# Dense single-pass products with unread results between the small products of TensorE

## The reference, cut to what matters

```
def step(S, inp):                       # one position, per head; S is 64 x 64
    r_t, w_t, k_t, v_t, a_t, b_t = inp
    sa = einsum('bhij,bhj->bhi', S, a_t)
    S = S * w_t + sa * b_t + v_t * k_t
    return S, einsum('bhij,bhj->bhi', S, r_t)
...
mu, var = mean(y), mean((y - mu)**2)    # over the 64 values of a head
y = (y - mu) * rsqrt(var + GN_EPS) * lnx_w + lnx_b
out = (y + bonus) * g                   # g = sigmoid(gd) @ gate_g2
```

## Time and profile before

| | us |
|---|---|
| median of 3 runs (lowest, highest) | 1946.46 (1945.67, 1948.81) |
| the profiled execution | 1947.46 |
| its span, first to last instruction | 1945.7 |
| TensorE busy | 1786.3 (92%) |
| VectorE busy | 973.9 (50%) |
| ScalarE busy | 484.3 (25%) |
| GpSimd busy | 271.0 (14%) |
| mean granted clock | 0.943 |

### The profile page before, as it was taken

One profiled execution on the slowest core, in us unless ns is written; L12 is line 12 of the kernel. 1 busy time (PEld: TensorE's weight loads), 2 busy tenths in 40 slices (PEclk: granted clock), 3 DMA queues, 4 the chain that ended last, 5 costly groups with the idle time before them and its releaser, 6 DMA issues. The chain is left out here.

```text
span 1945.7 us, 39461 instructions
## 1 busy us (share of the span) xinstructions
PE 1786.3 (92%) x17306; PEld 1601.8 (82%) x17306; DVE 973.9 (50%) x1730; ACT 484.3 (25%) x937; POOL 271.0 (14%) x357
## 2 busy tenths in 40 slices
PE   5999998997999758889979999999999999999996
PEld 4999994665666427888729999999999999999996
DVE  6233316775766385444344266445455455455455
ACT  6122113553222342222134321111111111111113
POOL 1000004324766030001011200000000000000000
PEclk8999998997999869999579999999999999999999
DMA  8211103102766200000042111110110111110203
GB/s 241 55 44 44 42 27 93 50 17 62 239 201 203 66 1 3 4 4 20 1 148 65 34 33 38 49 55 28 50 55 28 56 48 33 55 41 22 62 25 111
DMA packets 136613, 119.29 MB, mean 61 GB/s; under 512 B 16771, under 2 KB 123640, under 8 KB 136171
## 3 DMA queue, kind: packets, MB, share of 16 engines
q1 hardware_dynamic: 124507, 78.06, 13.6%
q0 software_dynamic: 11792, 38.17, 6.1%
q10 hardware_dynamic: 144, 0.52, 0.1%
HBM read 102.94 MB, written 11.44 MB: 59 GB/s over the span
## 5 line engine op out<-in xcount | busy, mean ns | idle before, releaser
L205 PE MATMUL bank<-normed2T_hi,w_hi 128*128 128x384 f32 (+1 forms) x1032 | 337.3, 327 | 0.0
L206 PE MATMUL bank<-normed2T_hi,w_lo 128*128 128x384 f32 (+1 forms) x1032 | 336.9, 326 | 0.0
L207 PE MATMUL bank<-normed2T_lo,w_hi 128*128 128x384 f32 (+1 forms) x1032 | 336.9, 326 | 0.0
L205 PEld LDWEIGHTS bank<-normed2T_hi,w_hi 128*128 128x128 f32 x1032 | 193.8, 188 | 1.6 <-issue 1.6
L207 PEld LDWEIGHTS bank<-normed2T_lo,w_hi 128*128 128x128 f32 x1032 | 193.8, 188 | 0.0
L206 PEld LDWEIGHTS bank<-normed2T_hi,w_lo 128*128 128x128 f32 x1032 | 193.8, 188 | 0.0
L205 PE MATMUL bank<-inner_hi,w_hi 128*128 128x384 f32 (+1 forms) x528 | 175.0, 331 | 10.2 <-DVE w_lo L494 7.1
L494 DVE TENSOR_TENSOR w_lo<-work,w_hi 128x1024 fp32r<-128x1024 f32 (+2 forms) x120 | 118.6, 989 | 130.6 <-ACT w_hi L489 129.4
L207 PE MATMUL bank<-inner_lo,w_hi 128*128 128x384 f32 (+1 forms) x528 | 174.7, 331 | 0.0
L206 PE MATMUL bank<-inner_hi,w_lo 128*128 128x384 f32 (+1 forms) x528 | 174.5, 330 | 0.0
L205 PE MATMUL bank<-normedT_hi,w_hi 128*128 128x384 f32 (+3 forms) x480 | 157.8, 329 | 5.6 <-DVE w_lo L494 5.6
(11 more groups left out here) (410 smaller groups left out, 3199.4 us busy)
## 6 DMA issues: line engine op xcount, KB each, us to landing
work<-in_w_up_dram SPq DMA_DIRECT2D x44, 512.0 KB, 3.9
work<-in_w_in_dram SPq DMA_DIRECT2D x19, 512.0 KB, 3.8
work<-in_w_down_dram SPq DMA_DIRECT2D x32, 256.0 KB, 2.7
residualT<-residual_spill SPq DMA_DIRECT2D x1, 4352.0 KB, 16.4
work<-in_x_prompt_dram SPq DMA_DIRECT2D x8, 512.0 KB, 5.6
residual_spill<-rwkv_streamsT SPq DMA_DIRECT2D x8, 512.0 KB, 4.4
work<-in_w_out_dram SPq DMA_DIRECT2D x8, 512.0 KB, 4.8
out_dram<-work SPq DMA_DIRECT2D x8, 512.0 KB, 2.7
```

What stands on the lines that cost most here:

```text
L205: pe.matmul(out, w[0], x[0], start=first, stop=False)
L206: pe.matmul(out, w[1], x[0], start=False, stop=False)
L207: return pe.matmul(out, w[0], x[1], start=False, stop=last)
```

## The change

A helper `keep_busy` issues `n` products of a dense 128 x 128 tile with 512 columns of the same tile in fp32r (single pass). Their results go to a PSUM bank that is free at that time and are overwritten before anybody reads it. The tile is filled once, by a copy on ScalarE at the start of the sample block; TensorE waits for it after the solve. In the sample part two such products go ahead of each product q of kinds 1 to 3 (18 places, 36 products), behind the wait for the bank and ahead of the other waits. In the mixing twelve go behind the first three gate products, ahead of the wait for the reciprocal, and one behind each of the nine spreading products. Nothing is removed or moved.

```
--- before.py
+++ after.py
@@ -205,6 +205,11 @@
             pe.matmul(out, w[0], x[0], start=first, stop=False)
             pe.matmul(out, w[1], x[0], start=False, stop=False)
             return pe.matmul(out, w[0], x[1], start=False, stop=last)
+
+        def keep_busy(pe, dense, bank, n):
+
+            for _ in range(n):
+                pe.matmul(bank[:, 0:512], dense[:, 0:P], dense[:, 0:512], start=True, stop=True, skip_group_check=True)
 
         def C(name):
             return con[:, CONST[name][0]:CONST[name][0] + CONST[name][1]]
@@ -2098,6 +2103,8 @@
             sem("sample_taken_act"), sem("sample_taken_dve"), sem("sample_values_spread"),
             sem("sample_states_added"), sem("sample_states_new"))
 
+        dense = lay("dense", RW + 768, 512, F32R)
+        s_dense = sem("dense_set")
         of_sequence = C("seq_of")[0:NS, :].unsqueeze(2).broadcast_to([NS, NB, HD])
 
         def s_taken(eng, q):
@@ -2131,6 +2138,7 @@
             @block.tensor
             def _(pe):
                 products(pe, sample_ops)
+                pe.wait_ge(s_dense, 1)
                 taken(pe, op(i8, "RT"))
                 for f in range(2):
                     taken(pe, op(i8, "AP", f))
@@ -2149,6 +2157,8 @@
                         rows, m = head(h)
                         x = zs.wu[:, h]
                         cols = slice(h * HD, (h + 1) * HD)
+                    if 1 <= what <= 3:
+                        keep_busy(pe, dense, b, 2)
                     if what == 0:
                         last = pe.matmul(b[rows, 0:NS], x[:, 0:HD], ident[:, 0:NS], start=True, stop=True)
                     elif what == 1:
@@ -2222,6 +2232,7 @@
 
             @block.scalar
             def _(act):
+                nc.scalar.copy(dense[:, :], con[:, 0:512]).then_inc(s_dense, 1)
                 take_act(act, sample_ops)
                 for q in range(18):
                     what, h = divmod(q, 6)
@@ -2307,6 +2318,7 @@
                 pe.wait_ge(g_sig, 2)
                 for j in range(3):
                     gate_product(j)
+                keep_busy(pe, dense, PS[0], 12)
                 pe.wait_ge(y_ri, 1)
                 for j, (m, c) in enumerate(jobs):
                     if j >= 2:
@@ -2314,6 +2326,7 @@
                     rows = slice(32 * c, 32 * c + 32)
                     pe.matmul(PS[3 + j % 2][:, 0:384], heads_in[rows, m, 32:], devs[rows], start=True, stop=True
                               ).then_inc(y_bc, 1)
+                    keep_busy(pe, dense, PS[0], 1)
                     if 3 <= j:
                         gate_product(j)
```

## The result

The changed kernel takes 1968.7 us (median of 4, 1964.18 to 1976.36) against 1946.31 (median of 4, 1945.67 to 1948.81): ratio 1.0117, 95% interval 1.008 to 1.0153, so 22.4 us slower. Forecast were 1950.0 with 1935 to 1967: the direction was right, the size was not, and the time lies 1.7 us outside the range. The right direction counts for little: the forecast was 3.5 us above the median of before, less than the 3.9 that the prediction itself calls just tellable from no change. The execution that was profiled took 1976.36 us (span 1974.5), 28.9 more than the profiled one of before, and was the slowest of the four; sizes read from it are those of a slow draw.

A forecast was written before the change was run, and what follows sets the result against it. It took TensorE, busy without gaps at half clock in the sample part, as the bound. Sample part +8.0 and mixing -5.5 made +2.5 on the profiled 1947.46 us, hence 1950.0, range 1935 to 1967.

The forecast's parts named there:

- The sample part: Products 6 to 17 at +6.7 us and products 18 to 23 with what follows at +1.3: +8.0 us.
- That the products of the sample part are path time: Sample part: TensorE is busy without waiting, so added products cannot hide in a wait and lengthen the path.
- I take it that the clock falls all the same, two groups later than now: Products 6 to 17: half clock returns despite the pairs; two more groups run at full clock, saving 1.9 us.
- The price of a pair: Two dense 512-column products cost 0.85 us at half clock or 0.45 at full, estimated by columns from 384-column products.
- I let the clock come back half way: Products 18 to 23: three turns at 0.85 + 0.1 us, three at 0.45 + 0.1, together 4.5, that is +3.1.
- the start of products 24 and 25 at full clock (-1.8): Sample part, up to the first new state: half of 3.68 us saved because the clock is back by then.
- Mixing, -5.5: Mixing: full clock in the second loop saves 6.7 us, less 1.2 for dense products overrunning their wait.
- The overrun: Mixing: twelve dense products take 2.7 us in a wait of 1.51, overrunning it by 1.2.
- The loop: Mixing's second loop: full clock after the twelve dense products, 9.2 us instead of 15.84, saving 6.7.
- Rival B: The mixing starts at half clock and stays there, +15.3 us on the forecast: 1965.3 us; chance 0.26.
- Rival C: The added products move no clock anywhere, in sample part or mixing: +17.0, 1964.5 us; chance 0.11.
- Rival A: Full clock holds through the sample part, 1.00 at 933.4 and up to 950: -9.8 with the mixing, 1937.7 us; chance 0.30.

The follow-up runs named there:

- mixing only: Changed kernel without the sample part's 36 dense products, the mixing's 21 kept: 1947.14 us, ratio 1.0006 against the kernel before.
- the other data: Changed kernel with the dense tile filled from mixed activations instead of constants: 1973.41 us, ratio 1.0129 against the kernel before.
- the five plain products: Fillers in the mixing's waits and ahead of product 0, plus 5 dense after the last gate product, 5 float32 at next block's start: 1936.32 us, ratio 0.9952.
- sample-only kernel: Changed kernel without the mixing's dense products, the sample part's 36 kept: 1968.9 us, ratio 1.0115 against the kernel before.

## Why the prediction was wrong

Two terms of the sum failed. The sample part was put at +8.0 us and alone costs 22.5 by the medians; the mixing was put at -5.5 and alone changes nothing that can be told (+0.8). By its steps, the profiled execution against the forecast of +2.5 us; measured +30.3 in the cut.

- **That the products of the sample part are path time** held: 37.3 us busy of 37.3.
- **"I take it that the clock falls all the same, two groups later than now"** failed in its second half. It fell 0.4 us after the first pair had begun, that is two groups earlier: the first two groups of before, at full clock, went to half (+1.85) instead of two more gaining (-1.9). In the eight profiles that have no products ahead of product 0 it fell 0.1 to 2.9 us after the last start of kind 0, with before at the late end (930.50, 933.4). Four of the eight have the pairs, and there it fell after 0.1, 0.5, 2.2 and 2.5 us: the pairs put it off in none. I had read the one moment that its trace shows as a property of the code.
- **The price of a pair** was mis-sized at half clock: 1.15 instead of 0.85. The step by columns was right (0.42 for one more); what was missing is 0.30 for the way into and out of the dense products, which the pitch inside an uninterrupted run cannot show. Twelve pairs at 1.15 and two groups at 0.93 are 15.7. With the pair that is ahead of product 18's start the row of the table has +16.9 where I had +6.7 and its share of the next step.
- **"I let the clock come back half way" in kind 3** failed: all six turns are at half, 1.56 instead of 0.75 on the mean, and the start of products 24 and 25 at full clock (-1.8) did not come. The small product is 0.41 of it, where I had 0.1: it had been read from products that overlap. +6.4 in that step, +7.5 with the pair ahead, where I had +1.3.
- **Mixing, -5.5.** The overrun was right (1.2 forecast, 4.88 - 3.71 = 1.17). The loop was wrong: I took the full clock for granted once twelve dense products had run, since groups of that size had held it before. But the earlier trace rows shows them at 0.50 too, 17.35 us busy of 17.80 from 998.30 on, so the reading that the clock was lost only where there is next to no such work was false. The dense products ran in a bunch ahead of the first spreading, and in all three profiles with this arrangement (changed 1024.3, mixing only 993.8, the other data 1021.6) the clock fell ahead of the fourth gate product, where the loop begins in earnest. That adds 1.3 and 1.6 where 6.7 were to be saved. That the loop can run at full clock is right: with 6, 2 and 4 products where TensorE waited, and no single ones, it did in all five profiles that have them; the last step shrank by 7.4 in four of them (in the fifth the five plain products follow). Why it fell there with sixteen products and not with twelve is not shown.
- **Rival B** (the mixing starts at half clock) took a little of it, 3.1 us. About half is the load of the head sums, which landed 4.7 us after its issue instead of 2.4 and held TensorE back by 1.5 us; the rest is a clock of 0.50 from 1000.4 to 1003.8, which came back by itself. In the sample-only kernel this step is as before, so neither is shown to come from the change. **Rival C** (no clock moved) is nearest to what happened, though the clock did fall earlier by two groups: forecast +17.0, and with 1.15 for the pair, the two lost groups and 1.56 a turn it is 15.7 + 7.5 + 1.2 + 1.3 + 1.6 = 27.3, and 30.4 with the 3.1. I gave it 0.11: its main rival term, the loop of the mixing, I had taken as settled.
- **Rival A** decides at 933.4, and there it was out, the clock having been 0.50 since 928.7. With ten products the clock was held, and even so the kernel was slower: my sum for A (12 x 0.45 for the pairs) bought the clock with two products a group, where five lost it in the profiled execution.

What stays open: why the clock falls at one moment and not a few us later in the same code (0.1 to 2.9 us behind kind 0). No run separates that from the part before.

## What to carry to other kernels

Put filler products only where TensorE truly waits, a few at each wait of a sparse stretch, and look in the profile whether the next steps start when they did: then they are free, and here a loop behind them ran at full clock (-0.4%). Ahead of work that is itself the path they cost more here than the clock was worth, even when they held it. And where a clock hangs on a moment, read several executions before taking its place in one trace for a property of the code.

## What the runs showed of the hardware

A busy TensorE can sit at 1.2 GHz for long: 40.9 us busy of 40.9 in the changed kernel, with two full 128 x 128 products of 512 columns in each 3.4 to 3.6 us. One stream of instructions can run at either clock: with five such products ahead of each group, the groups went at 2.4 GHz up to 932.3 us (2.63 us for one of kind 1), at 1.2 GHz for 41 us (4.63 for one of kind 1), and at 2.4 GHz again from 973.3, all in one execution and without a gap. With ten the clock was 1.00 from the first group to the last. Single-pass products of 512 columns cost 0.42 us each at half clock and 0.228 at full in a run, and 0.30 or 0.21 beyond that for each small run of them between plain float32 ones.
